# Norm sums of a three-layer transformer kernel: one float32 product with the ones, or two in the rounded kind

## The reference

```python
def _rms_norm(x, gain):
    xf = x.astype(jnp.float32)
    y = xf * lax.rsqrt(jnp.mean(xf * xf, axis=-1, keepdims=True) + RMS_EPS)
    return (y * gain.astype(jnp.float32)).astype(x.dtype)

def _per_layer_embedding(x, p_i, norm, w_gate, w_proj):
    gate = jax.nn.sigmoid(_rms_norm(x, norm) @ w_gate)
    return gate * (p_i @ w_proj)
```

## Time and profile before

| | |
|---|---|
| Median of 3 runs | 1018.0 us (1017.61 to 1018.62) |
| Span of the profiled execution, first to last instruction | 1016.1 us |
| PE busy, matmuls | 1009.5 us, 8506 instructions |
| PE busy, weight loads | 984.0 us |
| DVE busy | 791.3 us, 950 instructions |
| ACT busy | 642.6 us |
| POOL busy | 3.0 us, 9 instructions |
| Granted clock of PE | 1.00 of full speed in all stretches |
| DMA | 187 MB, 184 GB/s over the span |
| Constants, issue to landing | 10.1 us |

### The profile page before, as it was taken

The page is one execution under the profiler, slowest core; times in us unless marked ns, Lnnn a source line. Parts: engine busy times, 40 slices in busy tenths (PEclk is TensorE's granted clock), DMA queues, the critical chain, the costliest instruction groups (busy, mean ns, idle before and its releaser), DMA issues.

```text
span 1016.1 us, 21078 instructions
## 1 busy us (share of the span) xinstructions
PE 1009.5 (99%) x8506; PEld 984.0 (97%) x8506; DVE 791.3 (78%) x950; ACT 642.6 (63%) x886; POOL 3.0 (0%) x9
## 2 busy tenths in 40 slices
PE   9999999999999999999999999999999999999998
PEld 7898999899999999999999999999899999999998
DVE  6879876686666756999887777798986788777787
ACT  7667655565454446677786657676746677656673
POOL 0000000000000000000000000010000000000000
PEclk9999999999999999999999999999999999999999
DMA  9852654355555564634555555454442556555541
GB/s 345 273 183 76 215 187 147 124 185 194 178 200 200 179 243 140 218 131 165 211 204 208 192 190 206 166 193 166 166 166 84 202 213 208 196 191 201 198 149 67
DMA packets 30687, 186.99 MB, mean 184 GB/s; under 512 B 3746, under 2 KB 6659, under 8 KB 8996
## 3 DMA queue, kind: packets, MB, share of 16 engines
q1 hardware_dynamic: 29908, 185.02, 51.7%
q10 hardware_dynamic: 720, 1.11, 0.4%
HBM read 183.99 MB, written 1.34 MB: 182 GB/s over the span
## 4 chain that ended last, share of the span: by engine, by line
PE 98%; DMA 1%; DVE 0%; ACT 0%; SPq 0%; issue 0%
PE g L604 65%; PE d L604 32%; PE d L607 1%; DMA raw<-weights 1%; PE g L607 0%; DVE co_both L1772 0%; DVE w_lo L1772 0%; ACT co_both L1212 0%; ACT w_hi L1212 0%; DVE probs_m_lo L1772 0%; DVE x L1769 0%; DVE ple_mul L1766 0%; SPq L528 0%; SPq L525 0%; ACT ple_sig L1212 0%
## 5 line engine op out<-in xcount | busy, mean ns | idle before, releaser
L1772 DVE TENSOR_TENSOR w_lo<-raw,w_hi 128x2048 fp32r<-128x2048 f32 (+2 forms) x176 | 389.2, 2215 | 89.6 <-ACT w_hi L1212 88.8
L1212 ACT ACTIVATE w_hi<-raw 128x2048 fp32r<-128x2048 f32 (+1 forms) x174 | 326.2, 1878 | 142.2 <-PE g L604 85.1
L604 PE MATMUL g<-f_both,w_hi 128*128 128x256 f32 x1408 | 240.8, 275 | 0.0
L604 PEld LDWEIGHTS g<-f_both,w_hi 128*128 128x128 f32 x1408 | 211.9, 188 | 0.1
L604 PE MATMUL g<-f_both,w_lo 128*128 128x256 f32 x704 | 193.7, 275 | 0.0
L604 PE MATMUL d<-hid_hi,w_hi 128*128 (+1 forms) x528 | 145.2, 275 | 0.0
L604 PE MATMUL d<-hid_lo,w_hi 128*128 (+1 forms) x528 | 145.2, 275 | 0.0
L604 PE MATMUL d<-hid_hi,w_lo 128*128 (+1 forms) x528 | 145.2, 275 | 0.0
L604 PEld LDWEIGHTS g<-f_both,w_lo 128*128 128x128 f32 x704 | 132.1, 188 | 0.0
L604 PE MATMUL g<-x_both,w_hi 128*128 128x256 f32 x704 | 120.0, 275 | 0.0
L604 PEld LDWEIGHTS g<-x_both,w_hi 128*128 128x128 f32 x704 | 105.9, 188 | 0.1
(11 more groups left out here) (370 smaller groups left out, 1938.3 us busy)
## 6 DMA issues: line engine op xcount, KB each, us to landing
raw<-weights SPq DMA_DIRECT2D x168, 1024.0 KB, 4.8
bias_tab<-bias_dram SPq DMA_DIRECT2D x8, 192.0 KB, 7.0
x<-x_t ACTq DMA_DIRECT2D x4, 256.0 KB, 5.6
raw<-weights SPq DMA_DIRECT2D x4, 256.0 KB, 6.7
raw<-weights SPq DMA_DIRECT2D x2, 512.0 KB, 7.5
mem_t<-mem_t SPq DMA_DIRECT2D x1, 1024.0 KB, 9.1
out<-x SPq DMA_DIRECT2D x3, 256.0 KB, 2.2
hy_swap<-hy_qk SPq DMA_DIRECT2D x4, 128.0 KB, 6.1
```

The lines of the kernel that those rows point to most:

```text
L604: return pe.matmul(out, lhsT, rhs, start=start, stop=stop, skip_group_check=True)
L1212: return act.activation(out, in_, func, **kw)
L1772: return dve.tensor_tensor(out, a, b, ALU.subtract)
```

## The change

At nine of the twelve sums the product with the ones is made in `float32r`. GpSimd waits for `sq_total`, casts the folded sum to a rounded `hi`, subtracts to get `lo`, and raises `sq_split`; PE waits for that instead of `sq_total` and makes two products, ones x hi and ones x lo, into the same bank. `hi` and `lo` lie in place of the buffers that held the squares. GAINED, GATE1 and GATE2 keep the single float32 product (`plain_sum`). The tile of ones is no longer part of the constants that are loaded: GpSimd makes it as `float32r` from the identity matrix once the constants have landed, and PE waits for that ahead of MIX. The float32 users of ones read the same tile.

```diff
-C_IDENT, C_ONES, C_HALF, C_WIN, C_FREQ = 0, 128, 256, 384, 640
-N_CONST = 641
+C_IDENT, C_HALF, C_WIN, C_FREQ = 0, 128, 256, 512
+N_CONST = 513
...
+        SQ_AT = place["at"]
         sq = sb("sq", [2, 2 * T])
         sq_sum = sb("sq_sum", [2 * T])
+        sq_r = at("sq_r", SQ_AT, [2 * T], F32R)
+        sq_sum_r = at("sq_sum_r", SQ_AT + 4 * 4 * T, [2 * T], F32R)
...
+        ones_r = sb("ones_r", [P], F32R)
...
+        SUM_LO, SUM_HI = slice(0, T), slice(T, 2 * T)
...
-            def norm_sum(squares=SQUARES, bank=STAT):
+            def sum_of(to, total, first=True):
+
+                mm(to, ones_r[:], total[:, SUM_HI], first, False)
+                return mm(to, ones_r[:], total[:, SUM_LO], False, True)
+
+            def norm_sum(bank=STAT):
+
+                count.next(sq_total)
+                pe.wait_ge(sq_split, count.next(sq_split))
+                acquire(bank)
+                fill(bank, sum_of(D[bank][:, 0:T], sq_sum_r), full_dve, mean_done)
+
+            def plain_sum(squares=SQUARES, bank=STAT):
 
                 pe.wait_ge(sq_total, count.next(sq_total))
                 acquire(bank)
...
                     pe.wait_ge(got_const, 16)
+                    pe.wait_ge(ones_ready, 1)
                     norm_sum()
...
-            pe.wait_ge(sq_total, count.next(sq_total, 2))
+            count.next(sq_total, 2)
+            pe.wait_ge(sq_split, count.next(sq_split, 2))
             acquire(1)
-            mm(D[1][:, 0:T], ones, sq[:, 0, 0:T])
-            fill(1, mm(D[1][:, T:2 * T], ones, sq_sum[:, 0:T]), full_dve, mean_done)
+            sum_of(D[1][:, 0:T], sq_r)
+            fill(1, sum_of(D[1][:, T:2 * T], sq_sum_r, False), full_dve, mean_done)
...
+            pool.wait_ge(got_const, 16)
+            pool.tensor_scalar(ones_r[:], ident, 0.0, 1.0, ALU.mult, ALU.add).then_inc(ones_ready, 1)
+
+            def round_sum(n, squares=sq_sum, parts=sq_sum_r):
+
+                total, hi, lo = squares[:, 0:T], parts[:, SUM_HI], parts[:, SUM_LO]
+                pool.wait_ge(sq_total, n)
+                pool.tensor_copy(hi, total).then_inc(sum_rounded, count.one(sum_rounded))
+                pool.wait_ge(sum_rounded, count.sent[sum_rounded])
+                pool.tensor_tensor(lo, total, hi.bitcast(F32), ALU.subtract).then_inc(sq_split, 1)
+
+            MIX, MEMORY, MOBA, CROSS, GATED_FFN, HYENA, GAINED, FFN1, GATE1, GLA_IN, FFN2 = range(1, 12)
+            round_sum(MIX)
+            round_sum(MEMORY)
+            round_sum(MOBA, sq[:, 0, :], sq_r)
+            for n in (CROSS, GATED_FFN, HYENA, FFN1):
+                round_sum(n)
             pool.wait_ge(x_gated, 1)
...
+            for n in (GLA_IN, FFN2):
+                round_sum(n)
```

More of the change, by code:

```diff
@@ L257, in program @@
         ident = const[:, C_IDENT:C_IDENT + P]
-        ones = const[:, C_ONES:C_ONES + P]
+        ones = ones_r[:].bitcast(F32)
         half_ones = const[:, C_HALF:C_HALF + P]
@@ L385, in program @@
         x_hi_done, x_split = sem("x_hi_done"), sem("x_split")
+        sq_split = sem("sq_split")
         sq_done, sq_total, sq_for_pe, att_squared = sem("sq_done"), sem("sq_total"), sem("sq_for_pe"), sem("att_squared")
@@ L411, in program @@
             "got_const", "got_par", "got_conv", "got_mem", "got_bias", "got_small", "got_rope", "got_p", "got_gla", "got_swap", "got_kswap"))
-        still_ready = sem("still_ready")
+        still_ready, ones_ready = sem("still_ready"), sem("ones_ready")
         half_done, half_evicted = sem("half_done"), sem("half_evicted")
@@ L415, in program @@
         bias_stored, masked_row, out_stored = sem("bias_stored"), sem("masked_row"), sem("out_stored")
-        cleared = sem("cleared")
+        cleared, sum_rounded = sem("cleared"), sem("sum_rounded")
         act_own, dve_own, pool_own = sem("act_own"), sem("dve_own"), sem("pool_own")
@@ L979, in _ @@
             for j in range(4):
-                chunk("hy_in", j, j % U, HY, fresh=j == 0, between=lambda: norm_sum(GAIN_SQUARES, 2), at_k=3 if j == 2 else None)
+                chunk("hy_in", j, j % U, HY, fresh=j == 0, between=lambda: plain_sum(GAIN_SQUARES, 2), at_k=3 if j == 2 else None)
                 if j == 1:
@@ L1058, in embedding @@
                 for j in range(COUNT[f"gate{layer}"] - 1):
-                    chunk(f"gate{layer}", j, j % U, moving, fresh=j == 0, between=norm_sum, at_k=6 if j == 0 else None)
+                    chunk(f"gate{layer}", j, j % U, moving, fresh=j == 0, between=plain_sum, at_k=6 if j == 0 else None)
                 chunk_halves(f"gate{layer}", COUNT[f"gate{layer}"] - 1, moving)
@@ L2674, in constants @@
     c[i, C_IDENT + i] = 1.0
-    c[:, C_ONES:C_ONES + P] = 1.0
     c[:, C_HALF:C_HALF + P] = (i[:, None] // 64 == i[None, :] // 64)
```

## The result

| | before | after |
|---|---|---|
| median, us | 1018.06 (1017.61 to 1018.62, 4 runs) | 1025.02 (1023.59 to 1026.70, 4 runs) |
| ratio | | 1.007, 95% interval 1.0058 to 1.0082 |
| span of the profiled run, us | 1016.1 | 1024.7 |

The change makes the kernel 7.0 us slower. The four runs of after lie further apart than those of before, 1023.59, 1024.98, 1025.06 and 1026.70, and the mean granted clock of the four falls in the same order: 1.000, 0.998, 0.998, 0.997. The profiled run is the slowest of them, so its trace shows the clock's part at its largest.

A forecast was written before the change was run, and what follows sets the result against it. PE bounds the kernel, in flight 1009.5 of 1016.1 us. Waits lose 6.35 and products win 2.0, so +4.35 makes the span 1020.5; plus 1.9 gives 1022.4 us, range 1015.7 to 1025.5.

The forecast's parts named there:

- main step: At the norm sums, GpSimd's SBUF reads wait for DVE's two-input w_lo: 6.35 us lost in all, chance 0.60.
- The rival on the other side: GpSimd reads beside DVE unhindered, the pair fits every slack, 2.0 us won: 1016.0 us, chance 0.26.
- GpSimd was not slow: Rival: GpSimd is not held but slow, a pair takes 3.0 us: 1018.2 us, chance 0.09.
- the products did get cheap: Rival: products with the rounded ones cost 0.22 us instead of 0.11, nothing won: 1018.0 alone, chance 0.05.
- the one on the start: Sign: GpSimd's cast at FFN1 starts at about 492.2 by the old clock, not at 490.05.
- PE's idle stretches released by GpSimd: Sign: PE idles about 3.1 us before the GATED_FFN sum and 0.8 at each convolution FFN.
- The saving: Two rounded products replace one f32 product, 0.25 us saved each at eight sums: 2.0 us won.
- FFN1 and FFN2: Convolution FFNs: after w_lo GpSimd's pair makes PE 0.84 us later at each, together 1.68.
- GATED_FFN: Two w_lo back to back hold GpSimd's pair, in either order; PE starts 3.1 us later.
- MIX: First sum: the subtraction waits for w_lo until 20.57; PE goes on 0.90 us later.
- HYENA: At its sum, nothing lost if GpSimd is first, 0.67 us if second; half taken, 0.35.
- DVE's own delay by GpSimd (at most 0.9 per place) is hidden: At all places, DVE's delay of at most 0.9 us costs nothing, since behind these w_lo DVE waits for PE's sum.

The follow-up runs named there:

- no_reads: Changed kernel with GpSimd's cast and subtraction replaced by two memsets, waits kept, norms not computed: 1016.32 us, ratio 0.9985 to the kernel before.
- dve_waits: Changed kernel, but DVE waits after each of the nine folds until GpSimd's pair is through: 1020.78 us, ratio 1.0028 to the kernel before.
- cast_only: Changed kernel with GpSimd's subtraction and the remainder left out, one rounded product per sum: 1016.69 us, ratio 0.9987 to the kernel before.
- dve_splits: Changed kernel, but DVE makes cast and subtraction at the nine sums, GpSimd only the ones tile: 1018.50 us, ratio 1.0007 to the kernel before.
- mixed_no_gates: Changed kernel with pairs on GpSimd at MEMORY, MOBA, on DVE at CROSS, GATED_FFN, FFN1, GLA_IN, FFN2; other sums f32: 1016.80 us, ratio 0.9989.
- fold_rounded: Changed kernel, but DVE's last addition writes the rounded kind at all twelve sums; no pair, remainder left out: 1015.90 us, ratio 0.9980.
- filled: Changed kernel with 22 overwritten products in front of PE's wait for the sum at GATED_FFN: 1023.73 us, ratio 1.006 to the kernel before.
- mixed: Changed kernel with pairs on GpSimd at MEMORY, MOBA, on DVE at CROSS, GATED_FFN, FFN1, GATE1, GLA_IN, FFN2, GATE2; others f32: 1017.41 us, ratio 0.9994.

## Why the prediction was right, and where its sizes were off

The forecast was slower, 1022.4 us; measured are 1025.0, inside the range by 0.5 (the slowest of the four runs, 1026.70, lies above it). The main step, that GpSimd's reads are held by DVE's w_lo, is shown three ways: `no_reads` takes the read away, `dve_waits` the overlap, `cast_only` one of the two instructions. The rival on the other side, no hindrance, would have been 1016.0; `no_reads` shows that this is what the change would have been worth, 1016.3. GpSimd was not slow (with its handovers the pair holds DVE up for 1.32 in `dve_waits`, against 1.11 assumed), and the products did get cheap.

Of the signs that the prediction named, the one on the start did not come in the form given: GpSimd's cast at FFN1 starts 0.06 after the sum, while w_lo is running. But the two do not both keep their length, which was the condition for being wrong: the cast takes 2.40. PE's idle stretches released by GpSimd are there, 2.60 (3.1 foretold) and 0.68 (0.8). The step over the sum goes from 0.78 to 0.58 where PE doesn't wait (GATED_FFN in `dve_splits`).

By its own terms:

- The saving. 0.25 per product was taken, 0.20 is what real pairs won at GATED_FFN, FFN1, GLA_IN and FFN2 in `mixed_no_gates`. Of the prediction's "0.21 to 0.25" the lower end was right, 0.44 less two times 0.114. Behind a wait even this is not won: the first product after it takes 0.22 to the next in place of 0.12, and the pair saves 0.09 (FFN1: shift 7.76 at the sum, 7.67 behind it; FFN2 the same). This is why FFN1 and FFN2 add 0.75 each and not 0.59.
- FFN1 and FFN2: a wait of 0.84 was predicted at each; PE's sum is 0.84 later at FFN1 (shift 6.92 to 7.76). That it fits to the hundredth is luck: from w_lo's end to PE's start 1.11 was taken as three handovers of 0.06, a cast of 0.33 and a subtraction of 0.60; it was 0.26 for the rest of the cast, 0.72 for the subtraction and 0.13 for two handovers.
- GATED_FFN: 3.1 was predicted, the sum is 2.76 later (0.63 to 3.39). The cast is done between the two w_lo, and the subtraction ends 0.58 after the second. I had foreseen both orders and said that they come out alike; they do within 0.35.
- MIX: 0.90 predicted, 0.94 at the place ( 20.62, now 21.56), of which a third comes back before 31 us. CROSS: 0.32 predicted; PE's sum is 0.06 later (shift 0.72 to 0.78), since the second w_lo is pushed by 0.20 and the subtraction ends 0.60 behind it. Over the whole place the change is -0.02.
- HYENA: half of 0.67 was put at the sum. PE waits for nothing at it, and 0.13 goes at the gained sum behind it. The price fell on DVE, as the next rows show, beside the earlier trace rows:

```profile
412.68 0.40 POOL L2687 CAST sq_sum_r<-sq_sum 128x256 fp32r<-128x256 f32 x1 [182.15 <-DVE sq_sum L1789]
412.69 2.53 DVE L1792 TENSOR_TENSOR w_lo<-raw,w_hi 128x2048 fp32r<-128x2048 f32 x1
413.16 2.67 POOL L2689 TENSOR_TENSOR sq_sum_r<-sq_sum,sq_sum_r 128x256 fp32r<-128x256 f32 x1
415.15 3.29 DVE L1789 TENSOR_TENSOR gain_sq<-gain_sq 128x512 f32<-128x512 f32 x4
```

w_lo is 0.25 longer, and the four additions take 3.29 in place of 2.73, the first of them held while GpSimd's subtraction gets its turn. DVE is 0.8 later from there on, and some 48 us further PE waits 0.73 for hy_probs_t. The same wait of 0.69 arises in `dve_splits`, where DVE makes the pair itself: it is DVE's lateness that counts.

Two steps failed. The first is the sentence "DVE's own delay by GpSimd (at most 0.9 per place) is hidden". It was read at FFN1, where DVE waits for PE, and carried over to all places. At HYENA it cost 0.81 and at GLA_IN 0.46 (+0.21 in place of -0.25). At MOBA the saving of 0.37 itself came back at v_tok. It comes back there in every variant of this study, also where nothing is added to DVE (`no_reads`, `fold_rounded`). The second is an omission: a wait of 3 us of PE was priced at 3 us. It took the clock with it, 2.9 us more in the profiled run and 1.3 in the median. Without the clock the profiled shift would be that of `filled`, 5.64 against 4.35. That the total came within 2.6 us owes something to terms that were too high (GATED_FFN 0.2, MIX 0.3, CROSS 0.1, HYENA's sum 0.2) and stood against those that were left out.

The Trainium skill, "SBUF — State Buffer", says in the section "Who interferes with whom" that a DVE instruction with two SBUF inputs contends with a GpSimd instruction that reads SBUF and not with one that only writes it, and in the section "SBUF: two separate sides" that whichever starts first keeps the other out for the whole instruction. This case's rows agree: casts of 2.39 to 2.41 beside a w_lo that was first and 0.40 beside none, memsets of 0.31 beside it, and a w_lo of 2.77 where GpSimd's subtraction was first.

## What to carry to other kernels

Moving a small read to an idle engine can cost what that engine waits for and not what the instruction takes: look at which instruction with two SBUF inputs runs at the moment of the handover, and count one of them per reading instruction. Where the bound engine has little slack, keep the pair on the engine that produced the data, at those places only where this engine is itself waited out, or take the second pass away altogether by letting the producer write the wanted kind (which here leaves the remainder out). A saving on the bound engine is worth nothing ahead of a place where the next engine is at its heels; walk the shift of each instruction against the kernel before to find these places, and price an idle stretch of TensorE of a few us with the clock it may lose.

## What the runs showed of the hardware that was not expected

- GpSimd's subtraction of 128x256 takes 0.74 and its cast 0.40 where nothing holds them; DVE needs 0.42 and 0.29 for the same two.
- The exclusion works in both directions. When GpSimd's read is first, DVE's w_lo of 2.29 becomes 2.53 (HYENA) or 2.77 (GLA_IN), and its second of two in a row 2.49 (GATED_FFN). And two w_lo in a row are not one block: GpSimd's waiting instruction gets in between, and the two take 4.69 in place of 4.49.
- After 2.60 us without a product TensorE ran at 1.2 GHz for about 6.8 us, and not after idle stretches of 0.68 and 0.89 in the same run. What exactly decides this was not tried; the times of the four runs suggest that the low stretch is not equally long in each.
- The first product of 128x256 after a wait takes 0.22 us to the next in place of 0.12. It is seen behind waits for GpSimd (FFN1, FFN2) and for DVE (0.22 at the w_lo near 696 in `mixed`), and in `cast_only` behind a delay of 0.04. So each of these waits cost 0.1 more than its length.
- An f32 product of 128x256 is 0.44 to 0.48 us of PE's time, and a rounded one 0.114: one of the rounded kind saves 0.35, two save 0.20.
